# Layer and RMS norms applied inside TensorE's transposes by diagonal matrices, with the roundings and remainders around them reordered

## The reference

```
def layer_norm(x, g, b):
    mu = mean(x); var = mean(square(x - mu))
    return (x - mu) * rsqrt(var + LN_EPS) * g + b

x = layer_norm(ALPHA * x + ffn, ln_ffn_g[l], ln_ffn_b[l])
```

## Time and profile before

| | us |
|---|---|
| runs | 1212.24, 1218.31, 1217.49 |
| median | 1217.49 |
| profiled execution | 1220.65 |
| its span, first to last instruction | 1218.8 |
| TensorE busy (products) | 1151.2 (94%) |
| VectorE busy | 617.4 (51%) |
| ScalarE busy | 457.6 (38%) |
| POOL busy | 221.7 (18%) |
| mean granted TensorE clock | 0.982 of full speed |

### The profile page before, as it was taken

One profiled execution on the slowest core, in us unless ns is written; L12 is line 12 of the kernel. 1 busy time (PEld: TensorE's weight loads), 2 busy tenths in 40 slices (PEclk: granted clock), 3 DMA queues, 4 the chain that ended last, 5 costly groups with the idle time before them and its releaser, 6 DMA issues.

```text
span 1218.8 us, 16391 instructions
## 1 busy us (share of the span) xinstructions
PE 1151.2 (94%) x6658; PEld 809.5 (66%) x6658; DVE 617.4 (51%) x880; ACT 457.6 (38%) x712; POOL 221.7 (18%) x194
## 2 busy tenths in 40 slices
PE   7999999999979998999999898999999889999998
PEld 6967644544338876644444346889887766998997
DVE  3696612222135777612122135884599884645544
ACT  3334411211033575411211025474565534434442
POOL 5500000000010000000000000487798541000000
PEclk9999899999999999799999999999999999999999
DMA  9488799999996346899999985453343332463560
GB/s 322 131 258 326 306 380 422 422 421 421 421 384 216 139 173 239 349 372 423 421 420 421 421 323 175 157 187 106 131 178 139 138 138 69 159 255 140 182 232 35
DMA packets 86885, 321.58 MB, mean 264 GB/s; under 512 B 7160, under 2 KB 18853, under 8 KB 62235
## 3 DMA queue, kind: packets, MB, share of 16 engines
q1 hardware_dynamic: 84064, 313.08, 66.5%
q0 software_dynamic: 2192, 7.23, 1.8%
q10 hardware_dynamic: 554, 0.22, 0.1%
HBM read 318.55 MB, written 1.96 MB: 263 GB/s over the span
## 4 chain that ended last, share of the span: by engine, by line
PE 68%; DVE 15%; ACT 6%; DMA 5%; POOL 2%; issue 2%; SPq 1%; DVEq 0%; ACTq 0%
PE bank L1703 33%; PE bank L1889 15%; PE bank L1962 8%; DMA arena<-in_moe_w_down_dram 5%; DVE w_lo L712 3%; POOL w_lo L712 2%; ACT w_hi L1113 2%; PE bank L1974 2%; PE bank L1880 1%; PE bank L1785 1%; SPq L844 1%; PE bank L1922 1%; DVE arena L3145 1%; DVE rows L3126 1%; DVE arena L3163 1%
## 5 line engine op out<-in xcount | busy, mean ns | idle before, releaser
L1113 ACT ACTIVATE w_hi<-ring 128x2048 fp32r<-128x2048 f32 (+1 forms) x102 | 191.7, 1883 | 199.1 <-PE bank L1703 199.0
L712 POOL TENSOR_TENSOR w_lo<-ring,w_hi 128x512 fp32r<-128x512 f32 (+1 forms) x124 | 178.3, 1471 | 438.2 <-ACT w_hi L1113 438.2
L712 DVE TENSOR_TENSOR w_lo<-ring,w_hi 128x2048 fp32r<-128x2048 f32 x71 | 161.8, 2283 | 147.0 <-ACT w_hi L1113 146.9
L1703 PE MATMUL bank<-x_hi,w_hi 128*128 128x256 f32 x680 | 113.9, 290 | 2.8 <-issue 2.8
L1703 PE MATMUL bank<-x_hi,w_lo 128*128 128x256 f32 x680 | 110.0, 284 | 3.3 <-POOL w_lo L712 2.1
L1703 PE MATMUL bank<-x_lo,w_hi 128*128 128x256 f32 x680 | 109.7, 284 | 0.8 <-DVE x_lo L2480 0.7
L1889 PE MATMUL bank<-ring,moe_x 128*64 128x512 f32 x336 | 99.4, 595 | 4.2 <-DMA arena<-in_moe_w_up_dram 2.7
L2781 DVE TENSOR_TENSOR y_r<-bank,y_r 128x512 fp32r<-128x512 f32 x32 | 22.1, 692 | 158.1 <-ACT y_r L1113 158.1
L1703 PE MATMUL bank<-w_hi,x_hi 128*128 128x512 f32 x320 | 92.7, 404 | 7.4 <-DVE x_lo L2603 2.9
L1703 PEld LDWEIGHTS bank<-x_hi,w_hi 128*128 128x128 f32 x680 | 94.6, 193 | 6.1 <-issue 5.6
L1703 PEld LDWEIGHTS bank<-x_hi,w_lo 128*128 128x128 f32 x680 | 94.0, 192 | 3.9 <-POOL w_lo L712 2.5
(11 more groups left out here) (371 smaller groups left out, 1719.7 us busy)
## 6 DMA issues: line engine op xcount, KB each, us to landing
ring<-in_moe_w_gate_dram SPq DMA_DIRECT2D x30, 1024.0 KB, 17.1
ring<-in_w_in_dram SPq DMA_DIRECT2D x15, 2048.0 KB, 8.1
arena<-in_moe_w_up_dram SPq DMA_DIRECT2D x26, 1024.0 KB, 16.9
arena<-in_moe_w_gate_dram SPq DMA_DIRECT2D x24, 1024.0 KB, 15.5
ring<-in_moe_w_up_dram SPq DMA_DIRECT2D x24, 1024.0 KB, 18.8
arena<-in_moe_w_down_dram SPq DMA_DIRECT2D x24, 1024.0 KB, 18.8
wslots<-in_moe_w_down_dram SPq DMA_DIRECT2D x24, 1024.0 KB, 22.2
ring<-in_w_mlp_up_dram SPq DMA_DIRECT2D x8, 2048.0 KB, 8.8
```

The costliest lines, as they stand in the source:

```text
L712: last = ops.tensor_tensor(part(w_lo, label, hb)[:, x].bitcast(F32R), ring_half(label, hb)[:, x], part(w_hi, label, hb)[:, x], ALU.subtract)
L1113: return s.activation(dst, src, ACT.Copy)
L1703: last = mm(bank(use_)[0:still.shape[1], at:at + cols], still, moving, start=start and opens and (hb, n, k) == (0, 0, 0), stop=stop and cl ...
```

## The change

At ln1, rm0 and rm1 the scaling by 1/std is taken from the rows and put into the transposes. VectorE makes a diagonal matrix per tile, the identity times the reciprocal (`diagonal`), and TensorE multiplies each 128x128 chunk of `xtok` by it (`norm_D`): a real product in fp32 in the place of a transpose, which comes out transposed and scaled. For ln1 the shift is added in the same banks: ahead of the statistics TensorE puts, for every chunk and tile, the product of one row of the shift with a row of ones there, and the diagonal products add to it. ln1 has no warm-up products any more; rm0 and rm1 keep theirs. ln3, the layer norm ahead of rm0, still makes whole rows.

The rows of ln1 are still wanted later, for the residual sum: `whole_tok` makes them on VectorE behind the remainder of ("k", 0). ScalarE rounds only the first half of the first block ahead of the jump and the second behind `second_tile`, which now waits for the last sums themselves and writes its unused output elsewhere. POOL makes half of the remainder of ("k", 0), waits for both subtractions, and makes the rest; its loads behind that wait for the subtractions too.

```
         y_hi, y_lo = y_r[:, 0, :], y_r[:, 1, :]
+        diag = again_(3 * BLK + 2 * NT * 2 * P + 2 * T, NT, P)
+        DIAGS = {"ln1": 0, "rm0": NT, "rm1": 2 * NT}
...
-        def low(eng, ops, label, hb, i=0, pieces=1):
+        def low(eng, ops, label, hb, i=0, pieces=1, pause=None):
...
             for j in range(pieces):
+                if pause is not None and j == pause[0]:
+                    eng.wait_ge(sem(pause[1]), NT)
...
-            low(pool, g, FIRST_BEHIND[0], 0, pieces=4)
-            for t in range(NT):
-                pool.wait_ge(sem("ln1_tok"), t + 1)
+            low(pool, g, FIRST_BEHIND[0], 0, pieces=4, pause=(2, "ln1_xhat"))
+            pool.wait_ge(sem("ln1_xhat"), NT)
...
             def second_tile(n):
                 at = int(n[2:]) // 2
-                act.wait_ge(sem("res_whole"), at + 1)
-                s.activation(xtok[:, 1, :], res[:, 1, :], ACT.Identity, accum_out=tile_sum).then_inc(sem("tile_sum"), 1)
+                unused = moe_x[:, 0, :]
+                for h in range(2):
+                    freed(act, ("sc", at, PAIRS - 1, 1, h))
+                s.activation(unused, res[:, 1, :], ACT.Identity, accum_out=tile_sum).then_inc(sem("tile_sum"), 1)
...
+                high(FIRST_BEHIND[at], 1)
...
-                highs(FIRST_BEHIND[l])
+                high(FIRST_BEHIND[l], 0)
...
                     over_pairs(act, over_copies)
+                    act.wait_ge(sem(f"over_steps{l}"), 4 * PAIRS * (ROUNDS - 1))
...
+            def norm_D(name, arrived, of, shift=None, before=0):
+
+                warm((name, 0), before)
+                for b in range(4):
+                    claim(pe, (name, b))
+                    for c in (2 * b, 2 * b + 1):
+                        for t in range(NT):
+                            if shift is not None:
+                                mm(bank((name, b))[:, c % 2 * T + t * P:c % 2 * T + (t + 1) * P],
+                                   shift[:, c * P:(c + 1) * P], ones[0:1, :], start=(c % 2, t) == (0, 0), stop=False)
+                for t in range(NT):
+                    pe.wait_ge(sem(arrived), of[t])
+                    pe.wait_ge(sem("diag"), DIAGS[name] + t + 1)
+                    for b in range(4):
+                        for c in (2 * b, 2 * b + 1):
+                            at = c % 2 * T + t * P
+                            last = mm(bank((name, b))[:, at:at + P], xtok[:, t, c * P:(c + 1) * P], diag[:, t, :],
+                                      start=shift is None and (c % 2, t) == (0, 0), stop=(c % 2, t) == (1, NT - 1))
+                        if t == NT - 1:
+                            full(last, (name, b))
...
             experts(0)
-            norm_T("ln1", xtok, "tok", 2)
+            pe.wait_ge(sem("rows1"), 32)
+            norm_D("ln1", "ln1_xhat", (1, 2), rows[1][0:1, 1, :])
...
-            norm_T("rm0", before=10)
+            norm_D("rm0", "ln3_tok", (1, 2), before=10)
...
-            norm_T("rm1", before=3)
+            norm_D("rm1", "mixed_in", (1, 2), before=3)
...
+            def diagonal(n, t):
+
+                link(v.reciprocal(rstd[:, t, 1:2], rstd[:, t, 0:1]))
+                v.tensor_scalar(diag[:, t, :], ident[:], rstd[:, t, 1:2], None, ALU.mult).then_inc(sem("diag"), 1)
...
+            def layer_norm_diag(n):
+
+                dve.wait_ge(sem("rows1"), 32)
+                for t in range(NT):
+                    mean_t(n, t)
+                    less_mean_t(n, t)
+                    dve.wait_ge(sem("ln_std"), NT * int(n[2:]) + t + 1)
+                    diagonal(n, t)
...
             def rms_norm(n):
                 for t in range(NT):
                     dve.wait_ge(sem("rms_std"), NT * ("rm0", "rm1").index(n) + t + 1)
-                    link(v.reciprocal(rstd[:, t, 1:2], rstd[:, t, 0:1]))
-                    v.tensor_scalar(res[:, t, :], xtok[:, t, :], rstd[:, t, 1:2], None, ALU.mult)\
-                        .then_inc(sem(f"{n}_xhat"), 1)
+                    diagonal(n, t)
...
-            layer_norm_tok("ln1")
+            layer_norm_diag("ln1")
             low_T("ln1")
             low(dve, v, ("k", 0), 1)
+            for t in range(NT):
+                whole_tok("ln1", t)
```

More of the change, by code:

```diff
@@ L1178, in second_tile @@
                 act.wait_ge(sem("tile_mean"), at + 1)
-                s.activation(xtok[:, 1, :], res[:, 1, :], ACT.Square, scale=-1.0, bias=mv[:, 1, 0:1],
+                s.activation(unused, res[:, 1, :], ACT.Square, scale=-1.0, bias=mv[:, 1, 0:1],
                              accum_out=mv[:, 1, 1:2]).then_inc(sem("ln_var"), 1)
@@ L2666, in _, with mean_t @@
                         tile_rows("ln0", t)
+            def diagonal(n, t):
+                link(v.reciprocal(rstd[:, t, 1:2], rstd[:, t, 0:1]))
+                v.tensor_scalar(diag[:, t, :], ident[:], rstd[:, t, 1:2], None, ALU.mult).then_inc(sem("diag"), 1)
+            def mean_t(n, t):
+                if t == 0:
+                    half_stats(t, 0)
+                    moments(n, t, half_stats(t, 1))
+                    dve.wait_ge(sem("ln_var"), NT * int(n[2:]) + t + 1)
+                else:
+                    dve.wait_ge(sem("tile_mean"), int(n[2:]) // 2 + 1)
@@ new lines, in less_mean_t, with whole_tok @@
+            def less_mean_t(n, t):
+                v.scalar_tensor_tensor(xtok[:, t, :], res[:, t, :], mv[:, t, 0:1], rows[1][:, 0, :], ALU.subtract, ALU.mult)\
+                    .then_inc(sem(f"{n}_xhat"), 1)
+            def whole_tok(n, t):
+                dve.wait_ge(sem(f"{n}_xhat"), t + 1)
+                v.scalar_tensor_tensor(xtok[:, t, :], xtok[:, t, :], rstd[:, t, 1:2], rows[1][:, 1, :], ALU.mult, ALU.add)\
+                    .then_inc(sem(f"{n}_tok"), 1)
+            def layer_norm_diag(n):
[5 more added lines that the diff above has]
+                    diagonal(n, t)
@@ L2668, in layer_norm_tok @@
             def layer_norm_tok(n):
-                r = rows[1]
                 dve.wait_ge(sem("rows1"), 32 * (int(n[2:]) // 2 + 1))
                 for t in range(NT):
-                    if t == 0:
-                        half_stats(t, 0).then_inc(sem("res_whole"), 1)
-                        moments(n, t, half_stats(t, 1))
-                    dve.wait_ge(sem("ln_var"), NT * int(n[2:]) + t + 1)
-                    v.scalar_tensor_tensor(xtok[:, t, :], res[:, t, :], mv[:, t, 0:1], r[:, 0, :], ALU.subtract, ALU.mult)\
-                        .then_inc(sem(f"{n}_xhat"), 1)
+                    mean_t(n, t)
@@ L2679, in layer_norm_tok @@
+                    less_mean_t(n, t)
                     dve.wait_ge(sem("ln_std"), NT * int(n[2:]) + t + 1)
                     link(v.reciprocal(rstd[:, t, 1:2], rstd[:, t, 0:1]))
-                    dve.wait_ge(sem(f"{n}_xhat"), t + 1)
-                    v.scalar_tensor_tensor(xtok[:, t, :], xtok[:, t, :], rstd[:, t, 1:2], r[:, 1, :], ALU.mult, ALU.add)\
-                        .then_inc(sem(f"{n}_tok"), 1)
+                    whole_tok(n, t)
             def rms_norm(n):
```

## The result

| | before | after |
|---|---|---|
| median of 10 runs each, same chip | 1217.4 us (1212.24 to 1219.7) | 1222.64 us (1218.48 to 1227.11) |
| ratio after / before, 95% interval | | 1.0049, 1.0034 to 1.0065 |
| profiled execution, its span | 1220.65, 1218.8 us | 1221.52, 1219.8 us |
| TensorE busy | | 1157.9 us |

The change costs 5.2 us, 0.43% by the medians and 0.49% by the ratio, which is estimated over all runs and is not the quotient of the medians. The forecast was 1220.0, +2.5 us: the time lies inside the range, at twice the predicted size.

The account below looks back on a forecast made before the run. The prediction took TensorE as the bound, busy 1151 of 1218.8 us. First norm +2.5, RMS norms -0.3 and +0.35, other edits 0, summed to +2.5 us: 1220.0 on the median, range 1212 to 1225.

Parts of the forecast that it names:

- The fetch gap stays: First norm: TensorE again waits about 5 us for instructions behind the overflow-loop branch, the refill standing behind the weight stream.
- rival A: First norm: the fetch gap goes or shrinks, by a shifted stream or DMA queue contents; -2.5 us, 1215.0 in all; chance 0.18.
- VectorE's chain: First norm: first subtraction 1.28 us instead of 2.43, second diagonal at 367.5; 3.2 us gone from the chain but not seen.
- the second diagonal: First norm: VectorE's 128x128 identity scaling for the second tile was to take 0.2 us, bounds 0.1 and 0.3.
- ScalarE's moved rounding: First norm: the rounding put behind the second root ends near 368.8, ahead of x_hi, and costs nothing.
- Passes: First norm: each fp32 product of 128 columns takes two passes; preamble 32, each tile 16 instead of 8.
- rival D: A real product takes four times a transpose; +8 us at the first norm, at least 2 at the others, 1228; chance 0.02.
- The clock recovers near 368.8: First norm: 12 preamble passes run before the clock recovers, 20 after, ending at 371.2; ScalarE starts at 373.8, +2.5 us.
- rival B: First norm: the clock stays low through the preamble until the first bank; +6.2 us, 1223.7 on the median; chance 0.12.
- RMS norms: Diagonals at the two RMS norms: -0.3 us ahead of the projections, +0.35 us ahead of the MLP.
- The rescaled rows left for later: 2.6 us of whole rows on VectorE behind its remainder of ("k", 0) fit its idle time; cost 0.
- The sum: Whole kernel: 2.5 - 0.3 + 0.35 = +2.5 us, giving 1220.0 on the median.

Follow-up runs that it names:

- experiment 8: Experiment 6 with SyncE's load of ("q", 0) moved behind the overflow loop and the first subtraction of the mean; 1215.98 us, ratio 0.9991.
- experiment 3: Changed kernel with TensorE counting up an unused semaphore 32 times at its start; 1222.87 us, ratio 1.006.
- experiment 4: Kernel before with TensorE counting up an unused semaphore 32 times at its start; 1217.09 us, ratio 0.9993.
- experiment 11: Experiment 8 with POOL's third piece waiting for both diagonals instead of the second subtraction; 1216.56 us, ratio 0.9999.
- experiment 6: Changed kernel with the whole shift brought in by products over all 128 rows, shift tile times identity; 1217.94 us, ratio 1.0016.
- experiment 5: Changed kernel with shift products over 128 rows times mean weights, adding only an eighth of the shift; 1217.17 us, ratio 1.0009.
- experiment 9: Changed kernel, one-row products kept, with the load of ("q", 0) started only after the first tile's mean is taken off; 1219.13 us, ratio 1.0015.
- experiment 2: Kernel before with diagonals in the two RMS norms only, first norm left as rows and transposes; 1217.23 us, ratio 0.9997.
- experiment 12: Experiment 11 with both RMS norms back to scaled rows and transposes; 1213.89 us, ratio 0.9989.
- experiment 10: Kernel before with the load of ("q", 0) started only after the first tile's mean is taken off; 1219.86 us, ratio 1.0016.

## Why the prediction came out as it did

*The fetch gap stays: right.* 5.12 us, ending 4.05 us after the mark. Its cause was half right. Waiting behind the weight stream is 2.6 us of it. The other 2.5 are the refill, of which 2.35 are there with empty queues too (experiment 8), where rival A had nothing left. Rival A's other mechanism, a stream moved by an instruction, did nothing even with 32 (experiments 3 and 4).

*VectorE's chain: right in all but one term.* The first subtraction took 1.28 us and not 2.43, and the diagonals were ready 6.7 us behind the mark at the latest (5.6 by the sum), unused until TensorE came. The one miss is the second diagonal: 1.32 us where I had 0.2, bounds 0.1 and 0.3. I had costed POOL's resumed pieces by their own reader, not by what they do to the VectorE instruction beside them. It was hidden here; experiment 11 shows it.

*ScalarE's moved rounding: right, cost 0.* It ended at 366.3, x_hi came at 375.95. *Passes: right.* Two for each product, 32 in the preamble, 32 for the tiles; rival D had no part in it.

*The step that failed: "The clock recovers near 368.8 ... 12 passes until then, the other 20 in 2.4 us, to 371.2".* I took the recovery time from the kernel before, where TensorE did 512-column products by 128 rows at that place. The change takes just these away and puts products of one row there. The clock stayed at 0.50 until 376.7, and x_hi came 6.5 us later than before, not 2.5. This is rival B, which I had at 6.2 us and a chance of 0.12. Experiments 6 and 5 give the counterproof: the same passes over 128 rows, and the first product is 2.5 us late by the identity and 3.0 by the mean weights. Experiment 9 shows that the 5 us gap is not needed: behind one of 2.38 us the clock fell under one-row products too, where behind 2.29 us it held under the others (experiment 8). That the time still fell inside the range is no merit of the sum: the range reached up to rival B, and B's mechanism is what happened.

*Why rival B was priced too low.* I weighed against it the rule of the Trainium skill (TensorE: Matmul & The Clock Gate, PE-mode transpose) on transposes, by which real products in their place should help. A real product of one row did not: in experiment 9 the clock fell under these products, in experiment 8 it did not under the others. The row that spoke for the rival, TensorE busy 4.38 of 5 us at 0.50, deserved more weight.

*RMS norms: right.* -0.27 and +0.29 against -0.3 and +0.35; experiment 2 repeats them.

*The rescaled rows left for later: right, 0.* They took 2.48 us, and VectorE still idled 1.45 us ahead of the remainder of ("q", 0). *The sum:* I added no give-back, and some 1.4 us came back at the second layer's experts, where the weight stream is the bound. That can be why rival B's total, 1223.7, was 1.1 above the 1222.64 measured, though 1.1 us is within the noise of a median.

What stays open: whether experiments 8, 11 and 12 beat the kernel before. At the norm they gain 1.8 to 2.2 us on it; the medians say 0.9, 0.7 and 3.4, the ratios 1.1, 0.1 and 1.3, and every interval holds 1. Open too is whether one-row products alone, with no pause of TensorE ahead of them, lower the clock.

## What to carry to other kernels

Where warm-up products give way to real work behind a stall, ask what the clock does under the new work, not how many passes it has: let small constants enter by products over all rows (a row of constants times ones is the same as the full tile of equal rows times the identity). A jump over a rarely taken loop costs a refill of the instruction stream, and a full weight stream in front of it doubled that here (5.12 us against 2.29); what is gained by emptying the stream is seen only if the engines behind the gap are ready. Compare executions from a mark close to the change, since the clock elsewhere moves the absolute times by more than the change does.

## What was not expected of the hardware

- Products of one row did not hold or bring back the clock of a busy TensorE: behind a gap of 2.38 us it fell from 1.00 to 0.50 at 363.4 us in experiment 9, where behind 2.29 us those over 128 rows left it at 1.00 (experiment 8). In the changed kernel the low clock lasted 13.7 us, with full-height products 6.8 (experiment 6). Once down, 128-row diagonal products back to back ran at 0.50 for another 5.4 us.
- With idle DMA queues TensorE still stood for 2.1 to 2.4 us behind the jump (experiments 8 to 12); in experiment 8 it went on 2.35 us after its packet moved.
- A 128x128 scaling on VectorE took 1.32 us beside POOL's remainder and 0.28 to 0.29 alone.
